# Spreading denominators and gate sums over the partitions: TensorE transposes replaced by a trip through DRAM

## What is computed

```python
def causal_block_attention(q, k, v, cum=None):        # groups A (cum=None) and C (gated)
    s = einsum('bqhd,bkhd->bhqk', qblk, k) * dk ** -0.5
    if cum_t is not None:
        s = s + cq[..., None] - cum_t[:, :, None, :]  # sums of log sigmoid forget gates
    s = where(kpos <= qpos, s, -inf)
    p = softmax(s, axis=-1)
    return einsum('bhqk,bkhd->bqhd', p, v)
# B: a dilated sliding window; D: a 128 key window, whose sink logit joins the denominator
mix = concatenate([oa, ob, oc, od], axis=-1)
h = x + mix @ w_o
return h + hierarchical_moe(rmsnorm(h, norm2_g), ...)
```

## Time and profile before

| what | us |
|---|---|
| median of 3 runs (lowest, highest) | 2005.02 (2003.66, 2007.26) |
| span of the profiled execution, first to last instruction | 2003.5 |
| PE busy in it | 1841.7 (92%) |
| DVE, ACT, POOL busy | 712.4, 555.0, 327.6 |
| DMA queue of SP (q1), share of 16 engines | 34.9% |

### The profile page before, as it was taken

One profiled execution on the slowest core, in us unless ns is written; L12 is line 12 of the kernel. 1 busy time (PEld: TensorE's weight loads), 2 busy tenths in 40 slices (PEclk: granted clock), 3 DMA queues, 4 the chain that ended last, 5 costly groups with the idle time before them and its releaser, 6 DMA issues. The chain is left out here.

```text
span 2003.5 us, 29201 instructions
## 1 busy us (share of the span) xinstructions
PE 1841.7 (92%) x11200; PEld 1013.5 (51%) x11200; DVE 712.4 (36%) x2085; ACT 555.0 (28%) x1313; POOL 327.6 (16%) x372
## 2 busy tenths in 40 slices
PE   7999998999899889998699999899998997999992
PEld 4555555776645443333255555567675554433330
DVE  0111105667634522222212221266764443222224
ACT  2121216665612211110121111266563222111010
POOL 0332321011100011111013332310210000111110
PEclk9999998999999989999899999999999997999996
DMA  7000000002061289999752110100203315999997
GB/s 262 11 22 11 0 21 32 1 1 96 2 260 64 105 318 415 423 417 416 277 176 84 43 53 0 53 2 1 85 12 129 147 64 215 356 422 422 415 364 305
DMA packets 93208, 325.73 MB, mean 163 GB/s; under 512 B 19856, under 2 KB 33808, under 8 KB 76688
## 3 DMA queue, kind: packets, MB, share of 16 engines
q1 hardware_dynamic: 70416, 272.97, 34.9%
q0 software_dynamic: 12096, 33.57, 4.2%
q10 hardware_dynamic: 10560, 17.33, 2.5%
HBM read 295.52 MB, written 38.80 MB: 167 GB/s over the span
## 5 line engine op out<-in xcount | busy, mean ns | idle before, releaser
L437 PE MATMUL banks<-r_win,r_tile 128*128 128x384 f32 (+3 forms) x1536 | 531.4, 505 | 9.4 <-DMA r_win<-in_w_in 7.2
L437 PEld LDWEIGHTS banks<-r_win,r_tile 128*128 128x128 f32 x1536 | 292.7, 192 | 226.8 <-issue 61.6
L1827 PE MATMUL banks<-r_win,r_proj 128*32 128x512 f32 (+2 forms) x1184 | 255.3, 606 | 7.9 <-DVE r_proj L2148 4.3
L1675 PE MATMUL banks<-r_proj,r_tile 128*128 128x512 f32 x512 | 238.2, 607 | 0.2 <-DVE r_proj L2098 0.2
L1107 ACT ACTIVATE r_win<-r_win 128x256 f32<-128x256 f32 (+7 forms) x256 | 177.3, 695 | 28.3 <-DVE r_win L1179 20.7
L1827 PE MATMUL banks<-r_proj 128*32 128x512 f32 (+1 forms) x736 | 157.1, 596 | 8.7 <-DMA r_win<-in_w 3.8
L990 PE MATMUL banks<-r_win 64*128 64x512 f32 (+3 forms) x704 | 136.1, 506 | 19.6 <-DVE r_win L1151 10.3
L1675 PEld LDWEIGHTS banks<-r_proj,r_tile 128*128 128x128 f32 x512 | 93.1, 193 | 94.2 <-issue 93.7
L1001 PE MATMUL banks<-fixed,r_win 128*128 128x128 f32 x984 | 132.4, 280 | 6.6 <-ACT r_win L1115 6.5
L1001 PEld LDWEIGHTS banks<-fixed,r_win 128*128 128x128 f32 x984 | 106.2, 141 | 49.5 <-issue 42.8
L507 ACT ACTIVATE r_proj<-banks,rx 128x384 f32<-128x384 f32 (+1 forms) x80 | 48.1, 601 | 297.2 <-PE banks L437 297.2
(11 more groups left out here) (229 smaller groups left out, 2114.9 us busy)
## 6 DMA issues: line engine op xcount, KB each, us to landing
r_win<-in_w SPq DMA_DIRECT2D x99, 1024.0 KB, 18.5
r_proj<-in_w SPq DMA_DIRECT2D x60, 1024.0 KB, 21.6
r_tile<-in_w SPq DMA_DIRECT2D x33, 1024.0 KB, 19.0
r_win<-in_w_in SPq DMA_DIRECT2D x6, 1536.0 KB, 18.3
r_proj<-in_w_o SPq DMA_DIRECT2D x2, 4096.0 KB, 13.4
residual<-r_tile ACTq DMA_DIRECT2D x16, 512.0 KB, 2.9
out<-r_tile SPq DMA_DIRECT2D x16, 512.0 KB, 8.2
r_win<-expert_rows SPq DMA_DIRECT2D x16, 512.0 KB, 9.7
```

Of the source, the lines that this page charges most:

```text
L437: mm = pe.matmul(bk[b][:, 0:CHUNKS[c]], uT[j][:, k, :], w_ch[c][:, k, :], start=(k == 0), stop=(k == KT - 1))
L1675: mm = pe.matmul(bk[2 * (t % 2) + c][:, :], mix[t][:, k, :], s.w_o[:, k, 512 * c:512 * c + 512], start=(k == 0), stop=(k == KT - 1))
L1827: mm = pe.matmul(bk[2 + j][at, 0:2 * F].rearrange("p (c n) -> p c n", c=2), xT[j][:, k, at], w13[c][:, :, k, :], start=(k == 0), stop=(k = ...
```

## The change

The two spreads over partitions no longer use PE, the ring, or `r_s` as a widened table.

- **Denominators.** DVE inverts into a ring of four slots (`rden`). SP stores the 128x8 inverses of a half to a DRAM tensor `denominators` in the order of queries (1024 elements, each a run of 4 bytes), waits until they have landed, and loads each head's 512 numbers back, broadcast to 64 partitions (two DMAs of 128 KB). ACT copies bank 7 unscaled to `mixT` (`heads_done`, which also sets `on`), and POOL multiplies that part of `mixT` in place by the loaded table (`normalise`).
- **Gate sums.** After step 3 SP stores `cum` to DRAM (4096 runs of 4 bytes) and, when pair 2 starts, loads it four times (512 KB each) broadcast to 128 partitions, straight into `cum_keys`. `spread_cum` and `cum_out` go.
- **Order.** SP's waits are now listed step by step. The last half's spread (n = 15) is issued in `route_experts`, behind the router's weights; POOL scales n = 14 and n = 15 there, PE waits for n = 14 before the fourth part of tile 0's projection and for n = 15 at tile 4, and DVE waits for n = 15 at `evac_hT(1)`.

```diff
@@ def plan_ring
-        ring += [("cum", key, "v") for key in cum_at(st)]
         ring += [("qk", key, "v") for key in heads_at(st)]
-        ring += [("norm", key, "a") for key in norm_at(st)]
@@ def attend
+    def spread_denominators(sp, pair, half):
+        n = 2 * pair + half
+        kept = s.den_dram[layer, n]
+        sp.wait_ge(g.rd.sem, g.rd.at(layer, n + 1))
+        sp.dma_start(kept.rearrange("j b q -> q (j b)"), rden[:, 2 * (pair % 2) + half, :],
+                     allow_slow_non_contiguous=True).then_inc(g.dw.sem, 16)
+        sp.wait_ge(g.dw.sem, g.dw.at(layer, 16 * (n + 1)))
+        if n >= 2:
+            sp.wait_ge(g.nm.sem, g.nm.at(layer, n - 1))
+        for j in range(2):
+            sp.dma_start(spread_to(n)[HD * j:HD * (j + 1), :],
+                         kept[j].rearrange("b q -> (b q)").partition_broadcast(HD)).then_inc(g.dr[n % 2].sem, 16)
+
+    def normalise(pool, pair, half):
+        n = 2 * pair + half
+        mine = mixT[:, 2 * MIXER_OF[pair // 2] + pair % 2, HALF * half:HALF * (half + 1), :]
+        pool.wait_ge(g.on.sem, g.on.at(layer, n + 1))
+        pool.wait_ge(g.dr[n % 2].sem, g.dr[n % 2].at(layer, 32 * (n // 2 + 1)))
+        nc.gpsimd.tensor_tensor(mine, mine, spread_to(n).rearrange("p (t n) -> p t n", n=P),
+                                ALU.mult).then_inc(g.nm.sem, 1)
@@ sync
+        for st in steps:
+            if st.k == 0 and st.pair == 2:
+                sp.wait_ge(g.cw.sem, g.cw.at(layer, 16))
+                sp.wait_ge(g.pv.sem, g.pv.at(layer, last_of(1)))
+                for h in range(HEADS):
+                    sp.dma_start(cum_keys[h // 2][h % 2].rearrange("p (t n) -> p t n", n=P),
+                                 s.cum_dram[layer, :, h].partition_broadcast(P)).then_inc(g.cu[h].sem, 16)
+            if st.k == 0 and st.pair == 4:
+                sp.wait_ge(g.pv.sem, g.pv.at(layer, last_of(3)))
+                sp.dma_start(s.w_o, s.ins["w_o"][layer].rearrange("(k p) n -> p k n", p=P)).then_inc(g.wo.sem, 16)
+            if st.k == 0 and st.pair == 5:
+...
+            if st.i == FOX_AT:
+                sp.wait_ge(g.rv.sem, g.rv.at(layer, emptied(ring_at["fox", 0], "v")))
+                sp.dma_start(s.cum_dram[layer].rearrange("t h p -> p (t h)"), cum.rearrange("p t h -> p (t h)"),
+                             allow_slow_non_contiguous=True).then_inc(g.cw.sem, 16)
+            for pair, half in norm_at(st):
+                spread_denominators(sp, pair, half)
@@ tensor
-            for key in cum_at(st):
-                spread_cum(*key)
-            for pair, half in norm_at(st):
-                spread_norm(pair, half)
@@ gpsimd
         for st in steps:
             for pair, half in norm_at(st):
-                widen(pair, half)
+                if 2 * pair + half < 2 * PAIRS - 2:
+                    normalise(pool, pair, half)
+            for pair, j in cum_at(st):
+                within_blocks(pair, j)
@@ scalar
+        def heads_done(pair, half):
+            act.wait_ge(g.pv.sem, g.pv.at(layer, step_of(pair, HALF * (half + 1) - 1).i + 1))
+            nc.scalar.activation(mixT[:, 2 * MIXER_OF[pair // 2] + pair % 2, HALF * half:HALF * (half + 1), :],
+                                 O.rearrange("p (t n) -> p t n", n=P), ACT.Copy).then_inc(g.on.sem, 1)
@@ route_experts
+            s.spread_denominators(sp, PAIRS - 1, 1)
```

More of the change, by code:

```diff
@@ L787, in cum_at @@
 def cum_at(st):
-    return [(st.pair + 1, st.k // 2, st.k % 2)] if (st.pair + 1) // 2 == 2 and st.k < 4 else []
+    return [(st.pair + 1, st.k)] if (st.pair + 1) // 2 == 2 and st.k < 2 else []
 def heads_at(st):
@@ L909, in _ @@
         sp.dma_start(causal, s.consts["causal"]).then_inc(g.causal.sem, 16)
[L910 to L917, removed]
+        for st in steps:
[9 more added lines that the diff above has]
+            if st.k == 0 and st.pair == 5:
+                sp.wait_ge(g.mx.sem, g.mx.at(layer, items_to(last_of(4) - 1)))
+                for x in range(2):
+                    for j in range(2):
+                        sp.dma_start(bias[x][:, 2 * P * j:2 * P * (j + 1)], s.consts["window"][2 * x + j]).then_inc(
+                            g.win[x].sem, 16)
+            if st.i == FOX_AT:
[4 more added lines that the diff above has]
+                spread_denominators(sp, pair, half)
     @block.tensor
@@ L955, in sum_fox @@
                                start=False, stop=(t == NT - 2))
[L956 to L971, removed]
             mm.then_inc(g.tp.sem, 1)
@@ L1072, in _ @@
             for pair, half in norm_at(st):
-                widen(pair, half)
-            for pair, j, half in cum_at(st):
-                if half == 1:
-                    if pair == 4 and j == 0:
-                        pool.wait_ge(g.causal.sem, g.causal.at(layer, 16))
-                    within_blocks(pair, j)
-        widen(PAIRS - 1, 1)
+                if 2 * pair + half < 2 * PAIRS - 2:
+                    normalise(pool, pair, half)
+            for pair, j in cum_at(st):
+                if pair == 4 and j == 0:
+                    pool.wait_ge(g.causal.sem, g.causal.at(layer, 16))
+                within_blocks(pair, j)
     @block.scalar
@@ L1139, in _ @@
             for pair, half in norm_at(st):
-                norm_out(pair, half)
+                heads_done(pair, half)
             if st.i == 0:
@@ L1631, in _ @@
         def _(pool):
+            for half in range(2):
+                s.normalise(pool, PAIRS - 1, half)
             pool.wait_ge(g.h.sem, g.h.at(layer, NT))
@@ L1673, in project_part @@
                     pe.wait_ge(g.h.sem, g.h.at(layer, t - 1))
+                if part == 3 and t % (NT // 2) == 0:
+                    normal = s.attend_sems.nm
+                    pe.wait_ge(normal.sem, normal.at(layer, 2 * PAIRS - 1 + t // (NT // 2)))
                 for k in range(k0, k0 + 2):
```

77 lines of the change are left out of this document (33 added, 44 removed).

## The result

The changed kernel takes 2050.15 us (median of 4 runs, 2038.75 to 2059.05) against 2004.34 us (2002.56 to 2007.26, 4 runs) of the kernel before on the same chip: a ratio of 1.023, 95% interval 1.019 to 1.026. It is slower by 46 us where 31 us of gain were forecast, and outside the range; it went the way of the rival on SP's trips. The profiled execution took 2047.1 us with a span of 2045.3.

The account below looks back on a forecast made before the run. PE sets the pace in attention. Terms 12.0 + 8.1 - 0.6 + 0.8 - 3.8 - 0.9 = 15.6 us per layer, 31 for both, take span 2003.5 to 1972.3; median 1.5 above: 1974 us, range 1960 to 1987.

Parts of the forecast that it names:

- the rival on SP's trips: SP's queue in attention: stores of 16.5 us hold SP 17.4 us per trip, trips back up; 2045 us, chance 0.05.
- part 4: The trip through DRAM: 3.4 us for a store, then two issues of 0.43 and 2.3 us for the load.
- The estimate of 2.0 us: Skill's fit for the 4 KB store, 2.0 us plus bytes over 436 GB/s; sum some 2 us better.
- Part 5: Pair 5, store of n = 7 queued behind `w_o`: PE's logits wait for DVE's maxima, -3.8 us per layer.
- Part 6: Barrier at attention's end waits for SP's trip of n = 14: -0.9 us per layer, between 0 and -2.6.
- Parts 1 to 3: Attention, per layer: removed transposes 12.0 us, PE's waits gone 8.1, window pairs take back 0.6, shorter end chain 0.8.
- parts 1 and 2: Attention, per layer: transposes removed from PE 12.0 us, PE's waits that go 8.1 us, collisions in window pairs -0.6.
- part 1: Attention, 24 transpose groups removed from PE at 0.50 us each: 12.0 us per layer, between 11.5 and 15.0.

Follow-up runs that it names:

- the turned kernel: Changed kernel, but DVE turns each half's block of inverses before SP stores it, as 128 runs of 128 bytes: 1975.21 us, ratio 0.984.
- The gate sums alone: Kernel before, with only the gate sums through DRAM (one store, four loads per layer), denominators staying with PE: 1993.97 us, ratio 0.994.
- runs of 32 bytes: Changed kernel, but a half's inverses are stored as 128 runs of 32 bytes, loads unchanged, so denominators are misplaced: 1975.14 us, ratio 0.984.
- both tables ahead: Changed kernel with 4-byte stores, but POOL makes both of pair 5's gate tables before scaling pair 3's second half: 2013.16 us, ratio 1.003.

## Why the prediction was wrong

The step that failed is part 4, "I take 1.9 + 1.5 = 3.4 us for a store". Everything else in the sum can be read off the kernels with runs of 32 or 128 bytes, which differ from the changed one in this price alone: 1975.1 and 1975.2 us against the forecast 1974.0. That checks the sum, not each term: only the gate sums were measured by themselves. The prediction had named a store landing after more than 5 us as what would make it wrong, and that is what happened.

- **Part 4, the price of a store.** Forecast 3.4 us, between 2.3 and 5.1; measured 10.6. The upper bound was the router's weights: 1024 runs of 16 bytes, the same number of runs, but those are read from DRAM and written to SBUF. The changed store writes to DRAM, and side by side. I took the number of runs for what sets the price, and with room between its writes the same store does take 3.6 us. The neighbourhood was the surprise, and no row of before had such a write, which the text said; it then bounded the price by rows of another direction. The 3.4 us were weak by themselves: 1.9 stands in no row shown, and the 1.5 by which the router's weights should end behind the tiles is by the trace of before about 1 (the tiles, issued at 551.3 and 551.6, land after 5.2 us, the weights, issued at 552.13, after 5.4). That is small beside the 7 us that were missing. The Trainium skill ("DMA: Bandwidth & Descriptors", Rules for kernel authors) had said to rearrange such a pattern rather than store it; the runs agree with the rule. The estimate of 2.0 us by the Trainium skill's fit on that page, which stood beside the sum, was a fifth of what was measured. The page gives that fit for DMAs issued by GpSimd, and these were issued by SP.
- **Part 5, behind `w_o`.** Forecast -3.8 us per layer, bounds -1.7 to -7.5. With a short store the wait is 3.2 to 3.5 us per layer, and taking it away, by moving `w_o` and the tables together, gave 1975.21 - 1965.65 = 9.6 us, 4.8 per layer. The mechanism and the place are right. In the changed kernel the loads come 21.5 us behind `w_o`'s issue (1454.01 to 1475.47) instead of 14.9, the whole trip being in front of the two tables. Pair 4 has a wait of its own that part 5 did not list, 6.95 us in layer 1; with pair 5's 11.34 that makes 18.3.
- **Part 6, the end of attention.** Forecast -0.9 us per layer, by "3.4 us for the store"; with short stores the barrier's wait is 0.9 to 2.2 us in each layer. In the changed kernel it is 16.7 and 19.2 us, three trips of 10 to 12 us in a row behind inverses that, by the stores of the turned kernel, come 7.4 and 4.6 us apart.
- **Parts 1 to 3, what is removed.** The gate sums alone gave 12.2 us. By parts 1 and 2 they were worth 16 groups x 0.50 = 8.0, their own waits of 0.7 and the ring's 1.7 x 2: 12.1 us. The rest of the 31.2 is 19.1 us for the denominators' part; measured from that kernel to the one with runs of 32 bytes, 1993.97 - 1975.14 = 18.8. PE's busy time fell by 20 us, not the 30 that I named as a sign: the groups' records had counted tails that the next matmul covers, which is why part 1 used slots (0.48 to 0.56 us a group) and not busy time (0.63). POOL's scaling takes 1.27 us, not 0.99, without a measurable cost. The price could be read before: the earlier trace rows is a multiply by a few numbers per partition repeated over columns, while the trace of before also has one by a full second table, which is what the new scaling is:

```profile
L668 POOL TENSOR_TENSOR r_proj<-r_proj,gain_a 128x512 f32<-128x512 f32 x16 | 20.3, 1271 | 1.3
```

- **The rival "SP's trips back up"** named the mechanism, the place and nearly the time (2045 us), but had a chance of 0.05, because its price was thought out of reach. Its deciding point, a store of about 11.5 us, was too high. It reckoned one row of four trips, n = 11 to 14, in the 33 us up to ACT's copy; on SP's timeline of layer 1 n = 11 is out of the way before n = 12 is stored (1523.83 and 1538.30), and the three left have only the 18 us from there to the end of PE's work at 1556.55. So the barrier's wait alone, at about 10.2 us for a store, already took back the gain (both tables ahead: ratio 1.003). With the tables queued behind a scaling on GpSimd the waits inside attention came on top, and 10.6 us were enough for 46 us of loss. That its 2045 us lie so near the measured time is luck: its store was 16.5 us.

What the 69.4 us between the spans of the changed kernel and the turned one (2045.3 and 1975.9) consist of: gated maxima 31.9 - 6.7 = 25.2, barrier 35.9 - 3.3 = 32.6, PE's busy time at a lower clock 1828.6 - 1821.1 = 7.5, waits for ACT's copies 11.0 - 6.6 = 4.4. That is 69.7. The last of these was not followed up: PE waits 3.9 us in each layer for ACT before pair 0's second transposes (before 3.3), and near the end of attention 2.5 more in layer 1 and 0.8 in layer 0.

## What to carry over

A cost that no row of the trace shows is to be bounded by a row that does the same thing in the same direction (who is read, who is written, what lies beside it), and where none exists, the case in which it lies above all bounds deserves more than 1 in 20, above all when a short chain of dependent trips stands on a queue in front of a barrier. Count such trips as a rate: a queue that holds each of them for 12 us cannot serve results that come 5 to 7 apart. And when a new wait enters an in-order engine, look at what is queued behind it: here, making two tables before the scaling was worth 37 us with the slow store and was free.

## What the runs showed of the hardware

- A store of 1024 4-byte runs that lie side by side in DRAM is reported as landed some 8 us after the DMA engines have finished with its packets (layer 0's first store), and no busy column shows it. The price follows how closely the separate writes lie: with 16 in each 64 bytes a store is waited for 10.6 us, with 4 it is 4.0, with one 3.6. It hardly depends on how many neighbourhoods there are (512 runs: 9.5) or on how many partitions send to one (two: 9.2). How large a neighbourhood is was not tried; 64 bytes is only the distance at which I looked.
- Turning the block on VectorE first takes 211 ns and buys 7.9 us per store (10.6 to 2.7).
- GpSimd's multiply of 128x512 takes 1.27 us where the second operand is a full table, in the kernel before as in the changed one, against 0.99 in the earlier trace rows, where numbers are repeated over columns.
- The output of attention decides the routing, and so the time: with denominators that sent the tokens to other experts the matmul records went from 11,008 to 13,008 and the time to 2310.95 us. Compare the number of matmuls before using the time of a variant that computes something else.
